# Softmax denominators in an attention phase: row sums over 64 partitions by one product, and their reciprocals on VectorE

## The chip, the cores and the metric
One Trainium2 chip, one of its cores. The metric is the device time of one execution of the whole program in microseconds (us), as the median of several runs.

## The reference, cut to what matters
Two blocks of a network on a sequence of 2048 tokens. The second block normalises x, projects it to q (8 heads of 64), k and v (2 heads of 64 each, shared by 4 query heads), gates and a convolution branch. The context of 256 tokens gives further keys and values, so each query sees 2304 keys. The change touches only this part:

```
s = jnp.einsum('bqkgd,bskd->bkgqs', qblk, k).astype(jnp.float32) * scale
pr = jax.nn.softmax(s, axis=-1).astype(v.dtype)
return jnp.einsum('bkgqs,bskd->bqkgd', pr, v)
```

All is float32. The softmax is taken as exp(s - max), weighted sum of v, and at the end a division by the sum of the exponentials (the denominator).

## The kernel before, in words
The program runs five phases one after the other, with a barrier between them: modulation, a gated linear attention block, the projections, `attention` (L1440) and the output. The change lies in `attention` alone.

The work of `attention` is 32 steps, one for a query head and a block of TB = 512 queries. A step goes over its 2304 keys in NKT = 18 turns of 128 keys. For step i, each engine runs a `body` of its own, whose instructions stand in an order written by hand, and semaphores tie the engines together:

- TensorE (`body`, L1623): each turn kt makes scores for 128 keys and 512 queries by two products (L1630, L1631) into one of three score banks. Between turns stand groups of other work. `piece` (L1590) makes four products of the scores of the NEXT step in the other orientation, in tokens by keys, only to find each query's maximum; there are 20 pieces in a step, five for each 128 queries (four of 512 keys and one of 256), and they stand in groups of four at the turns that PIECES_OF_TURN names. Pieces use 64 rows of the array each, so that two lie side by side. `weigh` (L1605) multiplies the exponentials with v into bank O, even keys into partitions 0 to 63 and odd ones into 64 to 127, three calls at each of the turns 9 and 14 and at turn 2 of the next step. `sum_den` (turn 5) and `spread_reciprocal` (turn 7) belong to the step before; `max_row` (turn 15) turns the maxima into a row.
- ScalarE takes the exponential of each turn's scores into p_f (L1694), copies half of O (L1682), rounds q and moves the row of maxima.
- VectorE finds maxima: `reduce` (L1726) reads one piece's bank and writes one column. Of the four banks M a group of pieces fills all; piece p waits, if p is even, until max(p - 2, 0) pieces of its step are reduced (`mx_read`, in `piece`). So the third piece of a group (p = 10 in the group at turn 9) waits for the whole group before it (p = 4 to 7). VectorE also adds the last of the sums of exponentials (L1743, L1747) and ends a step: `add_o` adds the two halves of O, `invert` takes the reciprocal, `finish` (L1762) multiplies and frees the output tile for a store by the SyncE queue.
- GpSimd adds the exponentials over the turns into den, seven tiles of 128x1024 a step by six additions (L1575).

Denominators before: `sum_den` has four products with a column of ones (L1613), one for each 128 queries, with the denominators in partitions and one column; `invert` (L1756) takes the reciprocal of 128x4 values; `spread_reciprocal` (L1620) turns each column, broadcast, into a row over 128 partitions with four transposes into O; `finish` reads that from O. The first `weigh` of a step waits for `o_done`, since O is free only when `finish` has read it.

Of the kernel before, what the change touches and what calls it, by code (L numbers as in the profile page):

```python
# [10 lines left out]
ALU = mybir.AluOpType  # L11
# [4 lines left out]
P = 128  # L16
SEQ, D = 2048, 1024
KT = D // P
TB = 512
NB = SEQ // TB  # L20
NT = TB // P
EPS = 1e-6
UP = 1
# [895 lines left out]
HD, NQH, NKV = 64, 8, 2  # L919
# [520 lines left out]
def attention(nc, d, keep):  # L1440
# [10 lines left out]
    STEPS = NKV * GROUP_STEPS  # L1451
    PIECES = [(qt, n) for qt in range(NT) for n in range(-(-KEYS // TB))]
    NP = len(PIECES)

    PIECES_OF_TURN = [0, 0, 4, 0, 4, 0, 0, 0, 0, 4, 4, 0, 0, 0, 4, 0, 0, 0]
    TURN_PIECES = [list(range(sum(PIECES_OF_TURN[:kt]), sum(PIECES_OF_TURN[:kt + 1]))) for kt in range(NKT)]
    assert sum(PIECES_OF_TURN) == NP
    with ExitStack() as ctx:
        sb, ps, sem = pools(nc, ctx, "att")
        ident = keep["ident"]  # L1460
# [4 lines left out]
        ones = sb("ones", [P, P])  # L1465
# [7 lines left out]
        p_f = sb("p_f", [P, NKT, TB])  # L1473
        den = [sb(f"den{s}", [P, 2, TB]) for s in range(2)]
        o_hi, o_out = sb("o_hi", [HD, TB]), sb("o_out", [HD, TB])
        recip = sb("recip", [P, NT])
        S = [ps(f"bank_s{i}", [P, TB]) for i in range(SBANKS)]
        M = [ps(f"bank_m{i}", [P, TB]) for i in range(MBANKS)]
        O = ps("bank_o", [P, TB])
# [7 lines left out]
            sem(n) for n in ("mx_done", "mx_read", "m_done", "mz_done", "row_done", "row_read"))  # L1487
        s_done, p_done, den_pool, den_dve, pv_done = (
            sem(n) for n in ("s_done", "p_done", "den_pool", "den_dve", "pv_done"))
        den_sum, o_hi_done, recip_done, r_row, o_sum, o_done, o_stored = (  # L1490
            sem(n) for n in ("den_sum", "o_hi_done", "recip_done", "r_row", "o_sum", "o_done", "o_stored"))

        def need(eng, semaphore, n):

            if isinstance(n, int) and n <= 0:
                return
            eng.wait_ge(semaphore, UP + n)
# [19 lines left out]
        with nc.Block() as block:  # L1517
# [60 lines left out]
            @block.tensor  # L1578
            def _(pe):
                def piece(i, s, g, p):  # L1580

                    qt, n = PIECES[p]
                    width = min(TB, KEYS - TB * n)
                    rows = slice(HD * (p % 2), HD * (p % 2 + 1))
                    if p == 0:
                        pe.wait_ge(q_hi_done, UP + i + 1)
                        need(pe, row_read, i)
                    if p % 2 == 0:
                        need(pe, mx_read, i * NP + max(p - MBANKS + 2, 0))
                    pe.matmul(M[p % MBANKS][:, 0:width], q_c[s][rows, P * qt:P * (qt + 1)], k_a[g][rows, TB * n:TB * n + width],  # L1590
                              start=True, stop=True).then_inc(mx_done, 1)

                def max_row(i):

                    pe.wait_ge(mz_done, UP + i + 1)
                    for qt in range(NT):
                        last = pe.transpose(M[0][0:HD + 1, P * qt:P * (qt + 1)], mz[:, qt, :], ident[:])
                    last.then_inc(row_done, 1)

                def weigh(i, s, g, j):  # L1600
                    pe.wait_ge(p_done, UP + i * NKT + 2 * j + 2)
                    if j == 0:
                        need(pe, o_done, i)
                    for half in range(2):
                        last = pe.matmul(O[HD * half:HD * (half + 1), :], v[g][:, 2 * j + half, :], p_f[:, 2 * j + half, :],  # L1605
                                         start=(j == 0), stop=(j == NPR - 1))
                    last.then_inc(pv_done, 1)

                def sum_den(i, s):
                    pe.wait_ge(den_dve, UP + (i + 1) * DVE_ADDS)  # L1610
                    pe.wait_ge(o_sum, UP + i + 1)
                    for qt in range(NT):
                        last = pe.matmul(O[:, qt:qt + 1], den[s][:, 0, P * qt:P * (qt + 1)], ones[:, 0:1], start=True, stop=True)  # L1613
                    last.then_inc(den_sum, 1)

                def spread_reciprocal(i):

                    pe.wait_ge(recip_done, UP + i + 1)
                    for qt in range(NT):
                        last = pe.transpose(O[:, P * qt:P * (qt + 1)], recip[:, qt:qt + 1].broadcast_to([P, P]), ident[:])  # L1620
                    last.then_inc(r_row, 1)

                def body(i, s, g, before, after):  # L1623
                    pe.wait_ge(row_read, UP + i + 1)
                    pe.wait_ge(q_lo_done, UP + i + 1)
                    pe.wait_ge(q_copied[s], UP + 32 * (i // 2) + 32)
                    for kt in range(NKT):
                        need(pe, p_done, i * NKT + kt - SBANKS + 1)
                        keys = slice(P * kt, P * (kt + 1))
                        pe.matmul(S[kt % SBANKS][:], k_a[g][:, keys], q_a[s][:], start=True, stop=False)  # L1630
                        pe.matmul(S[kt % SBANKS][:], k_b[g][:, keys], q_b[s][:], start=False, stop=True).then_inc(s_done, 1)  # L1631
                        if after is not None:
                            for p in TURN_PIECES[kt]:
                                piece(i + 1, 1 - s, after, p)
                        if kt == 2 and before is not None:
                            for j in GROUP_AT[kt]:
                                weigh(i - 1, 1 - s, before, j)
                        if kt in (9, 14):
                            for j in GROUP_AT[kt]:
                                weigh(i, s, g, j)  # L1640
                        if kt == 5 and before is not None:
                            sum_den(i - 1, 1 - s)
                        if kt == 7 and before is not None:
                            spread_reciprocal(i - 1)
                        if kt == 15 and after is not None:
                            max_row(i + 1)
                pe.wait_ge(ones_landed, UP + 16)
                pe.wait_ge(cleared, UP + 1)
                pe.wait_ge(k_hi_done, UP + 1)
                for p in range(NP):  # L1650
                    piece(0, 0, 0, p)
                max_row(0)
                pe.wait_ge(k_lo_done, UP + NKV)
                pe.wait_ge(v_landed, UP + 16 * NKV)
                pe.wait_ge(ones_row, UP + NKV)
                steps(pe, body)
                for j in GROUP_AT[2]:
                    weigh(STEPS - 1, 1, NKV - 1, j)
                sum_den(STEPS - 1, 1)
                spread_reciprocal(STEPS - 1)  # L1660

            @block.scalar
            def _(act):
# [50 lines left out]
            def _(dve):  # L1714
# [6 lines left out]
                def reduce(i, p):  # L1721
                    qt, n = PIECES[p]
                    dve.wait_ge(mx_done, UP + i * NP + p + 1)
                    if p == 0:
                        need(dve, m_done, i)
                    dve.reduce_max(mx[:, qt, n:n + 1], M[p % MBANKS][:, 0:min(TB, KEYS - TB * n)], AX_X).then_inc(mx_read, 1)  # L1726
# [25 lines left out]

                def invert(i):
                    dve.wait_ge(den_sum, UP + i + 1)
                    need(dve, r_row, i)
                    dve.reciprocal(recip[:], O[:, 0:NT]).then_inc(recip_done, 1)  # L1756

                def finish(i):
                    dve.wait_ge(r_row, UP + i + 1)
                    dve.wait_ge(o_sum, UP + i + 1)  # L1760
                    need(dve, o_stored, 16 * i)
                    dve.tensor_tensor(o_out[:], o_hi[:], O[0:HD, :], ALU.mult).then_inc(o_done, 1)  # L1762

                def body(i, s, g, before, after):
                    for kt in range(NKT):
                        if kt == 0 and after is not None:
                            split_q(i + 1, 1 - s)
                        if kt == 1 and before is not None:
                            add_den(i - 1, 1 - s, NPR - 1)
                            fold_den(i - 1, 1 - s)  # L1770
                        if kt == 4 and before is not None:
                            add_o(i - 1)
                        for n, p in enumerate(TURN_PIECES[kt]):
                            if after is not None:
                                reduce(i + 1, p)
                            if kt == 4 and n == 1 and before is not None:
                                invert(i - 1)
                        if kt == 4 and before is not None:
                            finish(i - 1)
                        if kt == 14 and after is not None:  # L1780
                            column(i + 1)
                        if kt == 17:
                            add_den(i, s, NPR - 2)
# [410 lines left out]
```

## Time and profile before
| | |
|---|---|
| median of 3 runs | 2878.21 us (2877.74 to 2882.36) |
| the profiled execution | 2884.46 us, of it a span of 2882.7 us |
| TensorE busy over the span | 90% |
| VectorE, ScalarE, GpSimd busy | 58%, 36%, 27% |
| the attention phase | about 1788 us to 2558 us of the span |
| one step in it | 23.3 us |

The span is the time between the first and the last instruction; what lies around it is 1.8 us. A timeline row has the start, the duration, engine, line, operation, out<-in, and the count of instructions merged in it; in brackets stands how long the engine was idle before, and what released it. A float32 product is two MATMUL records (a transpose is one), so `weigh` shows 12 records for six products. PEld is the load of weights, which runs beside PE.

### The profile page before, as it was taken

How to read it: one execution, taken by the hardware profiler on the slowest of the kernel's cores; microseconds unless marked ns; L12 is line 12 of the kernel's file. 1: busy time of each engine (PE TensorE's matmuls, PEld its weight loads, DVE VectorE, ACT ScalarE, POOL GpSimd, SP SyncE). 2: the span in 40 equal slices, each digit the busy share in tenths (PEclk: the TensorE clock that was granted, in tenths of full speed). 3: DMA queues.
4: the chain of work that ended last, by engine and by line, in shares of the span. 5: the costliest groups of instructions: out<-in, count | busy, mean ns of one | idle time of the engine just before them, and what ended most of it. 6: DMA issues, size and time to landing. Idle time of an engine off the chain costs nothing. (4 is left out here: it accounts for less than half of the span.)

```text
span 2882.7 us, 35232 instructions
## 1 busy us (share of the span) xinstructions
PE 2605.2 (90%) x11685; PEld 1754.7 (61%) x11685; DVE 1672.5 (58%) x2673; ACT 1044.2 (36%) x1830; POOL 765.5 (27%) x359
## 2 busy tenths in 40 slices
PE   8599899999999995699999993999999999947997
PEld 1177677777777774577777761444445544525776
DVE  0106542541542352488989866677777777746564
ACT  0234343343343331431313121445444444433332
POOL 0034321101111100003030112565556666631000
PEclk9799999999999997899999996899999999978999
DMA  8366578377567634557575654011111111033334
GB/s 318 106 220 196 184 246 287 126 251 257 189 215 249 215 126 159 194 182 261 186 252 185 225 177 101 23 28 29 32 29 28 28 28 28 24 121 114 120 131 146
DMA packets 233927, 433.54 MB, mean 150 GB/s; under 512 B 20513, under 2 KB 112151, under 8 KB 233552
## 3 DMA queue, kind: packets, MB, share of 16 engines
q1 hardware_dynamic: 207524, 337.48, 35.3%
q10 hardware_dynamic: 26284, 94.51, 9.5%
q8 instruction: 71, 1.16, 0.2%
q14 instruction: 48, 0.39, 0.0%
HBM read 326.77 MB, written 96.76 MB: 147 GB/s over the span
## 5 line engine op out<-in xcount | busy, mean ns | idle before, releaser
L1726 DVE TENSOR_REDUCE att_mx<-att_bank_m 128x1 f32<-128x512 f32 (+1 forms) x640 | 365.2, 629 | 114.1 <-PE att_bank_m L1590 110.3
L1694 ACT ACTIVATE att_p_f<-att_bank_s 128x512 f32<-128x512 f32 x576 | 317.9, 598 | 289.8 <-PE att_bank_s L1631 283.6
L456 PE MATMUL gla_bank_g<-gla_a_hi,gla_w_hi 128*128 128x512 f32 x1024 | 415.9, 406 | 5.2 <-POOL gla_w_lo L409 4.3
L456 PE MATMUL gla_bank_g<-gla_a_hi,gla_w_lo 128*128 128x512 f32 x1024 | 403.9, 394 | 0.0
L456 PE MATMUL gla_bank_g<-gla_a_lo,gla_w_hi 128*128 128x512 f32 x1024 | 403.5, 394 | 0.0
L1575 POOL TENSOR_TENSOR att_den<-att_den,att_p_f 128x1024 f32<-128x1024 f32 x160 | 378.9, 2368 | 36.3 <-ACT att_p_f L1694 24.2
L1342 DVE SCALAR_TENSOR_TENSOR proj_conv_acc<-proj_conv_in,proj_conv_w,proj_conv_acc 128x512 f32<-128x512 f32 (+1 forms) x480 | 353.1, 805 | 0.0
L1152 PE MATMUL proj_bank_g<-proj_u_hi,proj_w_hi 128*128 128x512 f32 x704 | 287.1, 408 | 3.7 <-DVE proj_u_lo L1330 3.7
L1152 PE MATMUL proj_bank_g<-proj_u_lo,proj_w_hi 128*128 128x512 f32 x704 | 274.3, 390 | 0.0
L1152 PE MATMUL proj_bank_g<-proj_u_hi,proj_w_lo 128*128 128x512 f32 x704 | 274.2, 389 | 0.0
L1605 PE MATMUL att_bank_o<-att_p_f,att_v 128*64 128x512 f32 x1152 | 270.1, 604 | 0.0
L1630 PE MATMUL att_bank_s<-att_q_a,att_k_a 128*128 128x512 f32 x576 | 258.7, 449 | 1.0 <-ACT att_q_b L1677 1.0
L1631 PE MATMUL att_bank_s<-att_q_b,att_k_b 65*128 65x512 f32 x576 | 230.3, 400 | 0.0
L456 PEld LDWEIGHTS gla_bank_g<-gla_a_hi,gla_w_hi 128*128 128x128 f32 x1024 | 195.1, 191 | 56.9 <-issue 14.3
L456 PEld LDWEIGHTS gla_bank_g<-gla_a_hi,gla_w_lo 128*128 128x128 f32 x1024 | 194.8, 190 | 42.8
L456 PEld LDWEIGHTS gla_bank_g<-gla_a_lo,gla_w_hi 128*128 128x128 f32 x1024 | 195.4, 191 | 38.2 <-issue 0.7
L1630 PEld LDWEIGHTS att_bank_s<-att_q_a,att_k_a 128*128 128x128 f32 x576 | 109.7, 190 | 137.0 <-issue 100.0
L827 DVE COPY gla_v_tok<-gla_bank_t 128x512 f32<-128x512 f32 x32 | 22.1, 691 | 260.7 <-PE gla_bank_t L563 260.7
L1152 PEld LDWEIGHTS proj_bank_g<-proj_u_hi,proj_w_hi 128*128 128x128 f32 x704 | 132.2, 188 | 55.3 <-issue 24.4
L1590 PE MATMUL att_bank_m<-att_k_a,att_q_c 64*128 64x512 f32 (+1 forms) x640 | 122.1, 435 | 47.9 <-ACT att_k_a L1666 44.9
L1605 PEld LDWEIGHTS att_bank_o<-att_p_f,att_v 128*64 128x64 f32 x1152 | 74.5, 137 | 146.0 <-issue 96.5
L402 POOL TENSOR_TENSOR gla_w_lo<-gla_w_raw,gla_w_hi 128x1024 fp32r<-128x1024 f32 x22 | 54.9, 2495 | 394.3 <-ACT gla_w_hi L622 394.3
(325 smaller groups left out, 4032.5 us busy)
## 6 DMA issues: line engine op xcount, KB each, us to landing
gla_w_hi<-scratch_w_hi SPq DMA_DIRECT2D x96, 512.0 KB, 4.2
gla_w_lo<-scratch_w_lo SPq DMA_DIRECT2D x96, 512.0 KB, 5.6
proj_w_hi<-scratch_w_hi ACTq DMA_DIRECT2D x90, 512.0 KB, 3.8
proj_w_lo<-scratch_w_lo ACTq DMA_DIRECT2D x90, 512.0 KB, 4.7
scratch_w_hi<-gla_w_hi SPq DMA_DIRECT2D x54, 512.0 KB, 4.4
scratch_w_lo<-gla_w_lo SPq DMA_DIRECT2D x54, 512.0 KB, 5.5
mod_wslab<-in_ada_w SPq DMA_DIRECT2D x6, 2048.0 KB, 11.3
mod_wslab<-in_w_mod SPq DMA_DIRECT2D x6, 2048.0 KB, 8.0
```

The lines of the kernel that those rows point to most:

```text
L402: pool.tensor_tensor(w2_lo[:], w_raw[m % 2][:], w2_hi[:].bitcast(F32), ALU.subtract).then_inc(w2_rest, 1)
L456: last = pe.matmul(banks[s % 2][:], w[:, k, :], a[:, k, :], start=(k == 0 and n == 0), stop=(k == KT - 1 and n == 2))
L827: dve.tensor_copy(v_tok[:, :, tok(j)], T[j % 2][:].rearrange("p (t i) -> p t i", t=NT)).then_inc(v_copied, 1)
L1152: last = pe.matmul(G[j % 2][:], w[:, k, :], a[half][:, k, :], start=(k == 0 and n == 0), stop=(k == KT - 1 and n == 2))
L1342: dve.scalar_tensor_tensor(acc, src, conv_w[:, c, k:k + 1], acc, ALU.mult, ALU.add).then_inc(taps, 1)
L1575: pool.tensor_tensor(den[s][:], pair(0) if j == 1 else den[s][:], pair(j), ALU.add).then_inc(den_pool, 1)
L1590: pe.matmul(M[p % MBANKS][:, 0:width], q_c[s][rows, P * qt:P * (qt + 1)], k_a[g][rows, TB * n:TB * n + width], start=True, stop=True).then ...
L1605: last = pe.matmul(O[HD * half:HD * (half + 1), :], v[g][:, 2 * j + half, :], p_f[:, 2 * j + half, :], start=(j == 0), stop=(j == NPR - 1))
L1630: pe.matmul(S[kt % SBANKS][:], k_a[g][:, keys], q_a[s][:], start=True, stop=False)
L1631: pe.matmul(S[kt % SBANKS][:], k_b[g][:, keys], q_b[s][:], start=False, stop=True).then_inc(s_done, 1)
L1694: act.activation(p_f[:, kt, :], S[kt % SBANKS][:], ACT.Exp, scale=float(HD) ** -0.5).then_inc(p_done, 1)
L1726: dve.reduce_max(mx[:, qt, n:n + 1], M[p % MBANKS][:, 0:min(TB, KEYS - TB * n)], AX_X).then_inc(mx_read, 1)
```

## The change
The sum over the 128 partitions of den is now one product with 64 columns of ones: every one of 64 partitions of O gets all 512 denominators as a row. The reciprocal is taken on this 64x512 tile, from O into an SBUF tile of that shape, and `finish` multiplies two SBUF tiles. The transposes are gone, and O is free for the next `weigh` once the reciprocal has read it (`recip_done` in place of `o_done`). The group of four pieces that stood at turn 4 stands at turn 5, directly ahead of the new product; the reciprocal stands between the second and the third reduction of that group, as before.

```diff
-    PIECES_OF_TURN = [0, 0, 4, 0, 4, 0, 0, 0, 0, 4, 4, 0, 0, 0, 4, 0, 0, 0]
+    PIECES_OF_TURN = [0, 0, 4, 0, 0, 4, 0, 0, 0, 4, 4, 0, 0, 0, 4, 0, 0, 0]
...
-        recip = sb("recip", [P, NT])
+        recip = sb("recip", [HD, TB])
...
                     if j == 0:
-                        need(pe, o_done, i)
+                        need(pe, recip_done, i)
...
-                    for qt in range(NT):
-                        last = pe.matmul(O[:, qt:qt + 1], den[s][:, 0, P * qt:P * (qt + 1)], ones[:, 0:1], start=True, stop=True)
-                    last.then_inc(den_sum, 1)
-
-                def spread_reciprocal(i):
-
-                    pe.wait_ge(recip_done, UP + i + 1)
-                    for qt in range(NT):
-                        last = pe.transpose(O[:, P * qt:P * (qt + 1)], recip[:, qt:qt + 1].broadcast_to([P, P]), ident[:])
-                    last.then_inc(r_row, 1)
+                    pe.matmul(O[0:HD, :], ones[:, 0:HD], den[s][:, 0, :], start=True, stop=True).then_inc(den_sum, 1)
...
-                        if kt == 7 and before is not None:
-                            spread_reciprocal(i - 1)
...
-                    need(dve, r_row, i)
-                    dve.reciprocal(recip[:], O[:, 0:NT]).then_inc(recip_done, 1)
+                    need(dve, o_done, i)
+                    dve.reciprocal(recip[:], O[0:HD, :]).then_inc(recip_done, 1)
...
-                    dve.wait_ge(r_row, UP + i + 1)
+                    dve.wait_ge(recip_done, UP + i + 1)
...
-                    dve.tensor_tensor(o_out[:], o_hi[:], O[0:HD, :], ALU.mult).then_inc(o_done, 1)
+                    dve.tensor_tensor(o_out[:], o_hi[:], recip[:], ALU.mult).then_inc(o_done, 1)
...
-                            if after is not None:
-                                reduce(i + 1, p)
-                            if kt == 4 and n == 1 and before is not None:
+                            if after is None:
+                                continue
+                            reduce(i + 1, p)
+                            if kt == 5 and n == 1 and before is not None:
                                 invert(i - 1)
-                        if kt == 4 and before is not None:
+                        if kt == 5 and before is not None:
+                            if after is None:
+                                invert(i - 1)
                             finish(i - 1)
```

On TensorE, in a step in the middle of the phase, from the scores of turn 4 on, the order was this before (att_bank_s are scores, att_bank_m pieces, att_bank_o is O):

```order
L1630 MATMUL att_bank_s<-att_q_a,att_k_a 128x512
L1631 MATMUL att_bank_s<-att_q_b,att_k_b 128x512
L1590 MATMUL att_bank_m<-att_k_a,att_q_c 128x256
L1590 MATMUL att_bank_m<-att_k_a,att_q_c 128x512 x3
L1630 MATMUL att_bank_s<-att_q_a,att_k_a 128x512
L1631 MATMUL att_bank_s<-att_q_b,att_k_b 128x512
L1613 MATMUL att_bank_o<-att_ones,att_den 128x1 x4
L1630 MATMUL att_bank_s<-att_q_a,att_k_a 128x512
L1631 MATMUL att_bank_s<-att_q_b,att_k_b 128x512
L1630 MATMUL att_bank_s<-att_q_a,att_k_a 128x512
L1631 MATMUL att_bank_s<-att_q_b,att_k_b 128x512
L1620 MATMUL att_bank_o<-ident_sb,att_recip 128x128 x4
```

and in the changed kernel, from the scores of turn 5 on, it is:

```order
L1621 MATMUL att_bank_s<-att_q_a,att_k_a 128x512
L1622 MATMUL att_bank_s<-att_q_b,att_k_b 128x512
L1590 MATMUL att_bank_m<-att_k_a,att_q_c 128x256
L1590 MATMUL att_bank_m<-att_k_a,att_q_c 128x512 x3
L1612 MATMUL att_bank_o<-att_den,att_ones 64x512
L1621 MATMUL att_bank_s<-att_q_a,att_k_a 128x512
L1622 MATMUL att_bank_s<-att_q_b,att_k_b 128x512
L1621 MATMUL att_bank_s<-att_q_a,att_k_a 128x512
L1622 MATMUL att_bank_s<-att_q_b,att_k_b 128x512
```

The four small products and the four transposes have become one product, directly behind the pieces and ahead of the scores of turn 6.

On VectorE the same stretch stood so before:

```order
L1747 TENSOR_TENSOR att_den<-att_den 128x512
L1726 TENSOR_REDUCE att_mx<-att_bank_m 128x1 x4
L1751 TENSOR_TENSOR att_o_hi<-att_bank_o,att_o_hi 64x512
L1726 TENSOR_REDUCE att_mx<-att_bank_m 128x1 x2
L1756 RECIPROCAL att_recip<-att_bank_o 128x4
L1726 TENSOR_REDUCE att_mx<-att_bank_m 128x1 x2
L1762 TENSOR_TENSOR att_o_out<-att_o_hi,att_bank_o 64x512
```

and now:

```order
L1735 TENSOR_TENSOR att_den<-att_den 128x512
L1714 TENSOR_REDUCE att_mx<-att_bank_m 128x1 x4
L1739 TENSOR_TENSOR att_o_hi<-att_bank_o,att_o_hi 64x512
L1714 TENSOR_REDUCE att_mx<-att_bank_m 128x1 x2
L1744 RECIPROCAL att_recip<-att_bank_o 64x512
L1714 TENSOR_REDUCE att_mx<-att_bank_m 128x1 x2
L1750 TENSOR_TENSOR att_o_out<-att_o_hi,att_recip 64x512
```

The places are the same; the reciprocal is of another shape, with two reductions of the group behind it.

## Rows read from the trace of the kernel before

**Rows 1.** Busy time over a stretch: PE, PEld, DVE, ACT, POOL, then granted clock
```profile
1811.00:2555.00 744.00, 734.47 (x3408) 367.78 (x3406) 559.91 (x896) 364.80 (x664) 452.64 (x192) 0.99 0.11 27
```

**Rows 2.** Timeline of one step, turns 4 to 10, PE and DVE
```profile
1952.21 0.72 PE L1590 MATMUL att_bank_m<-att_k_a,att_q_c 64*128 64x256 f32 x4
...
1953.44 0.95 PE L1613 MATMUL att_bank_o<-att_ones,att_den 128*128 128x1 f32 x8
...
1954.25 0.48 PE L1630 MATMUL att_bank_s<-att_q_a,att_k_a 128*128 128x512 f32 x1
...
1954.42 0.18 DVE L1756 RECIPROCAL att_recip<-att_bank_o 128x4 f32<-128x4 f32 x1 [0.78 <-PE att_bank_o L1613]
1954.52 1.28 DVE L1726 TENSOR_REDUCE att_mx<-att_bank_m 128x1 f32<-128x512 f32 x2
...
1955.04 0.39 PE L1631 MATMUL att_bank_s<-att_q_b,att_k_b 65*128 65x512 f32 x1
...
1955.27 0.60 PE L1620 MATMUL att_bank_o<-ident_sb,att_recip 128*128 128x128 f32 x4
1955.60 0.19 PEld L1630 LDWEIGHTS att_bank_s<-att_q_a,att_k_a 128*128 128x128 f32 x1
...
1956.72 0.73 PE L1590 MATMUL att_bank_m<-att_k_a,att_q_c 64*128 64x512 f32 x4
...
1957.38 2.79 PE L1605 MATMUL att_bank_o<-att_p_f,att_v 128*64 128x512 f32 x12
...
1958.29 0.14 PEld L1605 LDWEIGHTS att_bank_o<-att_p_f,att_v 128*64 128x64 f32 x2 [0.29 <-issue]
1958.72 0.14 PEld L1605 LDWEIGHTS att_bank_o<-att_p_f,att_v 128*64 128x64 f32 x2 [0.29 <-issue]
...
1960.11 0.50 PE L1630 MATMUL att_bank_s<-att_q_a,att_k_a 128*128 128x512 f32 x1
```

**Rows 3.** Groups of VectorE by shape: busy us, mean ns of one
```profile
L1756 DVE RECIPROCAL att_recip<-att_bank_o 128x4 f32<-128x4 f32 x32 | 5.9, 183 | 26.6 <-PE att_bank_o L1613 26.6
L162 DVE COPY cols<-mod_ps_cols 128x128 f32<-128x128 f32 x1 | 0.3, 292 | 11.6 <-PE mod_ps_cols L136 11.6
L1726 DVE TENSOR_REDUCE att_mx<-att_bank_m 128x1 f32<-128x256 f32 x128 | 53.3, 416 | 4.3 <-PE att_bank_m L1590 0.5
L1726 DVE TENSOR_REDUCE att_mx<-att_bank_m 128x1 f32<-128x512 f32 x512 | 327.9, 682 | 109.8 <-PE att_bank_m L1590 109.8
```

**Rows 4.** Timeline of TensorE around three pauses in an earlier phase
```profile
337.70 1.02 PE L594 MATMUL gla_bank_t<-ident_sb,gla_xrc 128*128 128x128 f32 x4 [2.45 <-DVE gla_xr L880]
...
354.94 0.76 PE L456 MATMUL gla_bank_g<-gla_a_hi,gla_w_hi 128*128 128x512 f32 x1 [2.03 <-POOL gla_w_lo L409]
355.50 0.63 PE L456 MATMUL gla_bank_g<-gla_a_lo,gla_w_hi 128*128 128x512 f32 x1
355.93 0.63 PE L456 MATMUL gla_bank_g<-gla_a_hi,gla_w_lo 128*128 128x512 f32 x1
...
601.35 0.63 PE L594 MATMUL gla_bank_t<-ident_sb,gla_xrc 128*128 128x128 f32 x4 [1.85 <-DMA gla_xrc<-in_x]
```

**Rows 5.** TensorE in stretches behind those pauses: busy, then granted clock
```profile
337.90:341.30 3.40, 3.40 (x11) 0.51 0.26 79
341.30:344.70 3.40, 3.40 (x16) 1.00 0.77 203
355.00:358.40 3.40, 3.40 (x8) 0.51 1.09 351
602.00:605.40 3.40, 3.40 (x16) 1.00 1.06 377
```

**Rows 6.** Timeline at the end of the phase, the last step's denominators
```profile
2556.96 0.68 DVE L1762 TENSOR_TENSOR att_o_out<-att_o_hi,att_bank_o 64x512 f32<-64x512 f32 x1 [1.21 <-PE att_bank_o L1620]
```

**Rows 7.** Timeline of GpSimd's additions and a small VectorE operation beside one
```profile
1965.41 2.35 POOL L1575 TENSOR_TENSOR att_den<-att_den,att_p_f 128x1024 f32<-128x1024 f32 x1
...
1966.51 1.28 DVE L1735 TENSOR_SCALAR att_mz<-att_m 128x4 f32<-128x4 f32 x1
```

More of the change, by code:

```diff
@@ L1489, in attention @@
             sem(n) for n in ("s_done", "p_done", "den_pool", "den_dve", "pv_done"))
-        den_sum, o_hi_done, recip_done, r_row, o_sum, o_done, o_stored = (
-            sem(n) for n in ("den_sum", "o_hi_done", "recip_done", "r_row", "o_sum", "o_done", "o_stored"))
+        den_sum, o_hi_done, recip_done, o_sum, o_done, o_stored = (
+            sem(n) for n in ("den_sum", "o_hi_done", "recip_done", "o_sum", "o_done", "o_stored"))
         def need(eng, semaphore, n):
@@ L1659, in _ @@
                 sum_den(STEPS - 1, 1)
-                spread_reciprocal(STEPS - 1)
             @block.scalar
```

## The prediction
> **What bounds the kernel now.** I read the busy times by engine first. Over the steady part of the attention phase TensorE is busy 734.5 of 744 us, VectorE 559.9, ScalarE 364.8, GpSimd 452.6, and the clock granted is 0.99 of full speed [rows 1]. So in this phase the order of work on TensorE sets the time. What TensorE no longer has to do comes off the end, 32 times; what another engine takes longer counts once TensorE has to wait for it. The second view is the timeline of one step [rows 2], which shows where the denominators stand between the scores, and when each wait would be met. The third are the groups of VectorE by shape [rows 3], for the price of the new reciprocal. The last are TensorE's pauses in an earlier phase and the clock behind them [rows 4, 5]. Below, all clock readings are those of the step in rows 2, whose four digits before the point I shorten (57.38 is 1957.38).
>
> **Removed from TensorE.** The four small products take a slot at 53.44 and the next scores start at 54.25: 0.81 us. The first score product behind such a change of work takes 0.48 in place of 0.39, so some 0.08 more: 0.89. The four transposes go from 55.27 to 55.60, 0.33, with the same 0.08 or so: 0.42. Together 1.31 us a step.
>
> **Added to TensorE.** One float32 product of 512 queries on 64 columns of ones has the form of one `weigh` product. Those run two side by side, and a pair of records starts every 0.43 us (58.29, 58.72); a product has two records, so a lone one occupies 0.86. The group of six takes from 57.38 to 60.11, 2.73, which is 6 x 0.43 and 0.15 for leaving that form of the array. So the new product costs 1.01 us. It cannot share the array with the pieces, which have 64 rows each where it has 128. Its weights are ones, 64 columns, and their load lies under the pieces.
>
> **Moved.** The group of pieces costs 0.66 us wherever it stands between scores (56.72 to 57.38), at turn 4 or 5, so the move alone is 0. ScalarE's exponentials are hidden: it is busy half the time, and four turns of scores in a row (6 to 9) are what turns 11 to 14 have already. TensorE alone would gain 1.31 - 1.01 = 0.3 us a step.
>
> **The times of the new order.** The four score products from 54.25 to 55.27 take 1.02 with the one 0.08: a turn of scores is 0.47. The pieces start one turn later than before, 52.21 + 0.47 = 52.68, and the product for the denominators at 53.34. The last of six `weigh` products ends 2.79 behind the first one's start, four slots of 0.43 less is 1.07 for a lone one: it ends at 54.41. The reciprocal starts then, where it did before (54.42). Scores of turns 6 to 9 follow from 54.35 on, and the pieces of turn 9 can start at 56.4, against 56.72 before.
>
> **The reciprocal.** This is the term that decides. The 128x4 one took 183 ns. A copy from PSUM of 128 columns took 292 [rows 3], and a reduction takes 682 for 512 columns and 416 for 256, so 1.04 ns a column; the copy's fixed part is 292 - 133 = 159 ns. The reciprocal is 24 ns above that for four columns. If that is a fixed part of its own, 512 columns take 183 + 508 x 1.04 = 0.71 us. If each column costs it, the price is 24/4 = 6.0 ns a column, and 512 take 0.16 + 3.07 = 3.23 us. With the reduction's fixed part (682 - 533 = about 150) in place of the copy's it is 33/4 = 8.25 ns and 4.37 us. I keep 0.71 and 4.4 as the ends and take 3.23: an engine that streams every other operation at the same fixed part has no reason to pay 24 ns once, and a copy out of PSUM is its nearest relative. 
>
> **What it holds up.** Two reductions stand behind the reciprocal on VectorE, those of the third and fourth piece of its group (1.28 us at 54.52). VectorE's next instruction starts 0.08 before the reported end of one (54.42 and 54.52 against 0.18). At turn 9 TensorE runs two pieces, and for the third it waits until all four of the group of turn 5 are reduced: 54.41 + R - 0.08 + 1.28 + 0.05 for the signal = 55.66 + R. The last two pieces take 0.44 of the 0.66, so `weigh` starts at 56.10 + R, against 57.38 before. At R = 1.0 us the reciprocal begins to hold up TensorE beyond its own gain, at 1.28 the change is even, and at 3.23 the step is 56.10 + 3.23 - 57.38 = 1.95 us longer. The wait of the first `weigh` for the reciprocal itself (57.6) is over by then, and moving it from `o_done` to `recip_done` gains nothing. VectorE has 5.9 us of idle time in a step of 23.3 [rows 1], so it catches up behind turn 10. Steps 1 to 30 have denominators and pieces at once: 30 x 1.95 = 58 us.
>
> `finish` now has both inputs in SBUF. A small VectorE operation on SBUF started at 66.51 and took 1.28 us, until GpSimd's addition (65.41, 2.35 us) was over [rows 7]. So `finish` may take up to some 2 us more, and hold back the reductions of turn 9; these are wanted only at turn 10, some 3.5 us later. I take 0, and 0.5 us a step as the upper end.
>
> **The clock.** TensorE now pauses in each step: the first two pieces of turn 9 end at about 56.9, the third starts at 58.9, so 2.0 us. In the earlier phase pauses of 2.45 and 2.03 us were followed by 3.4 us at a granted clock of 0.51, which is the 1.2 GHz level, and then full clock again; one of 1.85 us was followed by 1.00 [rows 4, 5]. At the lower level score-like products start every 0.43 us (355.50, 355.93) in place of 0.23 (55.04, 55.27), so 3.4 us of it lose 3.4 x (1 - 0.23/0.43) = 1.6 us. The new pause lies between these cases; I take six falls in ten, with none and all as ends: 30 x 0.6 x 1.6 = 29 us.
>
> **The ends.** The last step of the loop has no pieces; there `weigh` at turn 9 waits for the reciprocal (57.6 against some 56.7): 1 us. At the phase's end `finish` stood 1.21 us idle behind a reciprocal of 0.18 [rows 6]; these 1.39 us become 3.2: 1.8 us. Together 3.
>
> **Sum.** 58 + 29 + 3 = 90 us. The profiled execution took 2884.5 us, so it would be 2974; the median of the runs lies 6.3 below it, and against that median I say 2968 us. Differences of under 0.2% (6 us) can't be told from no change.
>
> **Rivals.**
> *The reciprocal costs over 8 ns a column* (4.4 us). For it speak the reduction's fixed part and the page's rule; against it the copy's. `weigh` comes 3.1 us later, 30 x 3.1 = 93; the pause is then 3.1 us and the clock falls nearly every time, 30 x 0.9 x 1.6 = 43; ends 5. About 3019 us.
> *The pauses cost no clock*: they end before it falls, as that of 1.85 us did. 58 + 3 = 61 us, 2939.
> *The reciprocal streams like any other operation* (0.71 us) and the 24 ns are paid once. Then `invert` and the two reductions end at 56.4, in time for everything, TensorE's own 0.3 us comes off 31 times, and the end loses a chain of transposes for 0.5 us of reciprocal, 0.9 us: about 10 us faster, 2868. This is the case of the other sign; it decides below R = 1.28 us. Only the smallness of 24 ns speaks for it.
>
> **How the numbers follow.** My forecast (3 to 3.6 us for the reciprocal, some of the falls of clock) has 0.42; over 8 ns a column 0.24; no fall of clock 0.17; streaming 0.17. The last one makes nearly all of the chance of faster, 0.13, and of no change, 0.04 (a gain of 10 us may come out as half); the other three make 0.83 of slower. The range need hold only these three: from 2925 (no falls and a reciprocal of 2.8 us, or so) to 3035 (4.4 us with a fall in each step).
>
> **What would show it.** In the changed kernel's profile: the reciprocal's mean time (0.7, 3.2 or 4.4 us); an idle time of TensorE ahead of the third piece of turn 9, released by VectorE's reduction, about 2 us in 30 steps; two MATMUL records of 64 columns and 0.43 us apart in place of eight and four; a granted clock in the phase under 0.99, near 0.95; and steps of 26 to 27 us in place of 23.3. The prediction is wrong if the reciprocal takes under 1.3 us, if the reductions come to stand elsewhere, or if the pause is followed by no or by many more low stretches of the clock.

## The result, and the profile after

The changed kernel takes 2982.03 us (median of 4 runs, 2980.59 to 2988.76) against 2880.07 us: 1.036 times the time before, with an interval of 1.034 to 1.038, so 102 us slower. The forecast was 2968, with a range of 2925 to 3035. The profiled execution has a span of 2987.0 us against 2882.7, 104.3 more.

VectorE's groups in the changed kernel, by shape (busy us, mean ns of one, idle before):

```profile
L1744 DVE RECIPROCAL att_recip<-att_bank_o 64x512 f32<-64x512 f32 x32 | 107.2, 3349 | 12.4 <-PE att_bank_o L1612 12.4
...
L1750 DVE TENSOR_TENSOR att_o_out<-att_o_hi,att_recip 64x512 f32<-64x512 f32 x32 | 46.2, 1443 | 0.1
```

The reciprocal answers to the 183 ns of [rows 3]. With 183 ns for 4 columns and 3349 for 512, a column costs 3166/508 = 6.2 ns; the forecast had 6.0 and 3.23 us.

One step, on TensorE and VectorE, from the pieces of turn 5 to the end of the pieces of turn 10 (it answers to [rows 2]):

```profile
1966.28 0.73 PE L1590 MATMUL att_bank_m<-att_k_a,att_q_c 64*128 64x256 f32 x4
...
1966.94 1.07 PE L1612 MATMUL att_bank_o<-att_den,att_ones 128*64 128x512 f32 x2
1967.94 0.50 PE L1621 MATMUL att_bank_s<-att_q_a,att_k_a 128*128 128x512 f32 x1
1968.05 3.35 DVE L1744 RECIPROCAL att_recip<-att_bank_o 64x512 f32<-64x512 f32 x1 [0.33 <-PE att_bank_o L1612]
...
1970.18 0.49 PE L1590 MATMUL att_bank_m<-att_k_a,att_q_c 64*128 64x512 f32 x2
1971.32 1.21 DVE L1714 TENSOR_REDUCE att_mx<-att_bank_m 128x1 f32<-128x512 f32 x2
1972.46 1.45 DVE L1750 TENSOR_TENSOR att_o_out<-att_o_hi,att_recip 64x512 f32<-64x512 f32 x1
1972.59 0.50 PE L1590 MATMUL att_bank_m<-att_k_a,att_q_c 64*128 64x512 f32 x2 [1.92 <-DVE att_mx L1714]
1973.02 4.49 PE L1605 MATMUL att_bank_o<-att_p_f,att_v 128*64 128x512 f32 x12
```

The new product keeps the next scores away from 66.94 to 67.94, 1.00 us (forecast 1.01). The first two pieces of turn 9 run at 70.18; the third waits at 72.59 for VectorE's reductions, which stand behind the reciprocal: TensorE is idle for 1.92 us (forecast 2.0). Then the six weighing products last 4.49 us against 2.79 in [rows 2]. The clock in these stretches (span, PE busy, PEld, DVE, ACT, POOL, then granted clock), with the mean over the phase first:

```profile
1850.00:2640.00 790.00, 726.05 (x2886) 318.95 (x2888) 641.49 (x847) 335.75 (x623) 425.00 (x177) 0.95 0.10 24
1965.00:1973.00 8.00, 6.08 (x24) 2.98 (x22) 6.66 (x7) 4.13 (x8) 6.73 (x3) 1.00 0.00 0
1973.00:1976.40 3.40, 3.40 (x12) 1.06 (x12) 3.03 (x5) 0.00 (x0) 3.04 (x2) 0.62 0.18 39
```

Full speed up to the pause, and a mean of 0.62 in the 3.4 us behind it, a mixture of the 1.2 and the 2.4 GHz level. I call such a stretch a fall of the clock. The record of the granted clock has one of 3.4 us in 26 of the 30 steps with a pause, and one more in the last step of the loop, which has no pieces and where the weighing waits 1.45 us for the reciprocal. The mean of 0.95 over 790 us says about the same (0.05 x 790 / 0.5 = 79 us at the lower level, 23 stretches, where the record has 25 in that window).

The start of turn 9's pieces, from step to step, gives the length of a step with a fall and of one without:

```profile
1997.24 0.49 PE L1590 MATMUL att_bank_m<-att_k_a,att_q_c 64*128 64x512 f32 x2
...
2024.24 0.50 PE L1590 MATMUL att_bank_m<-att_k_a,att_q_c 64*128 64x512 f32 x2
...
2049.59 0.50 PE L1590 MATMUL att_bank_m<-att_k_a,att_q_c 64*128 64x512 f32 x2
```

From 1970.18 to 1997.24 it is 27.06 us, from 2024.24 to 2049.59 it is 25.35, and 23.33 before. So a step is 2.02 us longer by the wait, and a fall costs 1.71 us more. 30 x 2.02 = 61 and 26 x 1.71 = 44 us give 105 us. The trace has the same: from the reciprocal of the first step with pieces to that of the last step of the loop, 30 steps on, it is 802.90 us (1833.03 to 2635.93) against 698.12 (1837.79 to 2535.91), 104.8 more. That is the difference of the spans within a microsecond.

### The profile page after: what moved, and what is told of

Same layout as the page of the kernel before. It is cut to its first block and busy times, and to the rows that moved or that the text cites. A ratio compares the mean times of both kernels' runs of the same rounds, so it can differ in the third digit from the quotient of the medians.

```text
span 2987.0 us, 34591 instructions
## 1 busy us (share of the span) xinstructions
PE 2652.3 (89%) x11365; PEld 1731.6 (58%) x11365; DVE 1792.1 (60%) x2673; ACT 1037.3 (35%) x1830; POOL 772.3 (26%) x359
## 5 line engine op out<-in xcount | busy, mean ns | idle before, releaser
L1682 ACT ACTIVATE att_p_f<-att_bank_s 128x512 f32<-128x512 f32 x576 | 311.1, 599 | 402.9 <-PE att_bank_s L1622 397.1
L1575 POOL TENSOR_TENSOR att_den<-att_den,att_p_f 128x1024 f32<-128x1024 f32 x160 | 387.4, 2422 | 132.5 <-ACT att_p_f L1682 120.4
L1605 PE MATMUL att_bank_o<-att_p_f,att_v 128*64 128x512 f32 x1152 | 313.2, 686 | 1.5 <-DVE att_recip L1744 1.5
L1590 PE MATMUL att_bank_m<-att_k_a,att_q_c 64*128 64x512 f32 (+1 forms) x640 | 131.3, 448 | 105.7 <-DVE att_mx L1714 60.9
L1605 PEld LDWEIGHTS att_bank_o<-att_p_f,att_v 128*64 128x64 f32 x1152 | 83.7, 153 | 171.3 <-issue 137.8
```

The lines of the kernel that those rows point to most:

```text
L1575: pool.tensor_tensor(den[s][:], pair(0) if j == 1 else den[s][:], pair(j), ALU.add).then_inc(den_pool, 1)
L1682: act.activation(p_f[:, kt, :], S[kt % SBANKS][:], ACT.Exp, scale=float(HD) ** -0.5).then_inc(p_done, 1)
```

## The experiments

All times are medians of several runs. The experiments were run in three sets, each on one chip and beside runs of the kernel before (2879.6 to 2880.2 us in each set). Ratios are to those runs, with their interval in brackets.

**A copy in place of the reciprocal.**

```diff
-                    dve.reciprocal(recip[:], O[0:HD, :]).then_inc(recip_done, 1)
+                    dve.tensor_copy(recip[:], O[0:HD, :]).then_inc(recip_done, 1)
```

> The reciprocal of 64x512 is replaced by a copy of the same shape, at the same place; the output is multiplied by the denominators in place of divided. Theory A (the reciprocal's 3.35 us on VectorE, ahead of two reductions of maxima, is the whole loss): a copy takes 0.69 us, the pause of TensorE in turn 9 goes, the granted clock in the phase is back at 0.99, and what is left is TensorE's own gain of 0.3 us a step: 2869 us, 2863 to 2876. Rival B (the new product, the moved group of pieces or the new waits cost by themselves): 2890 us or more.

Measured: 2876.81 us, ratio 0.999 (0.998 to 1.000), and the clock is back at full speed:

```profile
1830.00:2500.00 670.00, 662.20 (x2832) 300.72 (x2829) 562.23 (x839) 326.08 (x605) 421.58 (x174) 1.00 0.11 28
```

The loss is gone with the reciprocal; the rest of the change costs nothing on balance. But the gain left is 3 us, hardly clear of the noise, and not 11. A row of the same kernel shows what took part of it, in turns 6 to 9:

```profile
1975.66 0.40 PE L1621 MATMUL att_bank_s<-att_q_a,att_k_a 128*128 128x512 f32 x1
...
1976.20 0.19 PEld L1621 LDWEIGHTS att_bank_s<-att_q_a,att_k_a 128*128 128x128 f32 x1 [0.34 <-ACT att_p_f L1682]
1976.20 0.50 PE L1621 MATMUL att_bank_s<-att_q_a,att_k_a 128*128 128x512 f32 x1
```

The scores of turn 9 start 0.54 us behind those of turn 8, in place of 0.47, and take 0.50 in place of 0.40, since TensorE's stream was broken. What they wait for is ScalarE's exponential of turn 6, which ended at 1976.15. Some 0.15 of the 0.3 us a step are given back here (a step is 23.18 us against 23.33 before), so that 31 x 0.15 = 5 us of gain are left.

**The move of the pieces alone**, in the kernel before.

```diff
-    PIECES_OF_TURN = [0, 0, 4, 0, 4, 0, 0, 0, 0, 4, 4, 0, 0, 0, 4, 0, 0, 0]
+    PIECES_OF_TURN = [0, 0, 4, 0, 0, 4, 0, 0, 0, 4, 4, 0, 0, 0, 4, 0, 0, 0]
...
-                            if kt == 4 and n == 1 and before is not None:
+                            if kt == 5 and n == 1 and before is not None:
                                 invert(i - 1)
-                        if kt == 4 and before is not None:
+                        if kt == 5 and before is not None:
```

> The kernel before with only the group of pieces moved from turn 4 to turn 5, ahead of the four small products, and the reductions with it. Theory A: a group costs 0.66 us wherever it stands, so 2880 us, 2875 to 2886. Rival B (the move costs, by the reductions of turn 5 coming closer to the pieces of turn 9): over 2890 us, 0.4 us or more a step.

Measured: 2880.13 us, ratio 1.0002 (0.999 to 1.001). The move is worth nothing, as forecast.

**The reciprocal behind all four reductions.**

```diff
-                            if kt == 5 and n == 1 and before is not None:
+                            if kt == 5 and n == 3 and before is not None:
                                 invert(i - 1)
```

> The changed kernel with the reciprocal behind all four reductions of its group in place of between the second and third. Theory A (the third piece of turn 9 waits for reductions that stand behind the reciprocal): that wait goes, the first weighing product waits for the reciprocal itself in its place, 1.3 us later than in the kernel before against 2.0 now, and the pause is 1.5 us, too short for the clock to fall: 30 x 1.3 + 3 = 42 us over before, 2922 us; 2960 if the clock still falls. Rival C (it is the reciprocal's length between product and weighing that counts, wherever it stands): no difference from the changed kernel, 2982 us.

Measured: 2949.41 us, ratio 1.024 (1.022 to 1.025). That is between the two theories' numbers. The timeline shows the wait where theory A puts it:

```profile
2012.40 3.34 DVE L1744 RECIPROCAL att_recip<-att_bank_o 64x512 f32<-64x512 f32 x1
2013.75 0.73 PE L1590 MATMUL att_bank_m<-att_k_a,att_q_c 64*128 64x512 f32 x4
2015.87 1.61 DVE L1750 TENSOR_TENSOR att_o_out<-att_o_hi,att_recip 64x512 f32<-64x512 f32 x1
2015.88 4.49 PE L1605 MATMUL att_bank_o<-att_p_f,att_v 128*64 128x512 f32 x12 [1.40 <-DVE att_recip L1744]
```

All four pieces now run together, and the first weighing product waits 1.40 us for the reciprocal. But the clock fell nevertheless, here at this very step, and in every second one: 15 of 30, and once more in the last step. Behind the next step's pause, at 2042.24, it stayed up (busy times, then granted clock):

```profile
2016.00:2019.00 3.00, 3.00 (x10) 1.05 (x11) 3.00 (x5) 0.00 (x0) 2.92 (x2) 0.55 0.00 0
2043.00:2047.00 4.00, 4.00 (x18) 1.68 (x15) 3.82 (x7) 0.60 (x1) 2.98 (x2) 1.00 0.15 33
```

My expectation that so short a pause would cost no clock was wrong. What I had compared it with was a lone pause of 1.85 us in dense work [rows 4]; here four pieces stand directly ahead of it. But that isn't the whole of it: steps beside each other have the same pause of 1.40 us behind the same four pieces, one with a fall and one without, so neither the pause's length nor the work just ahead of it decides alone. What does, these runs don't tell.

**The pause filled with work**, in the changed kernel and in the one above. Four score products whose results are overwritten stand where TensorE pauses.

```diff
                             for n, p in enumerate(TURN_PIECES[kt]):
+                                if kt == 9 and n == 2:
+                                    pe.wait_ge(p_done, UP + i * NKT + 8)
+                                    for _ in range(4):
+                                        pe.matmul(S[1][:], k_a[g][:, 0:P], q_a[s][:], start=True, stop=True)
                                 piece(i + 1, 1 - s, after, p)
```

> The changed kernel with four more score products, whose results are overwritten, between the second and the third piece of turn 9, where TensorE pauses. They take 0.95 us of the 1.9. Theory A (a pause of about 2 us makes the clock fall, and 26 falls of 3.4 us cost 1.6 us each): the pause is cut to about 1 us, no falls, 2982 - 42 = 2940 us, 2934 to 2948, with more work done. Rival D (the falls cost nothing, since TensorE has time to spare, or don't come of this pause): 2982 us or more.

> The kernel of e3_behind (reciprocal behind all four reductions) with four more score products, results overwritten, between the pieces of turn 9 and the first weighing product, where TensorE pauses for 1.4 us. Theory A: what e3_behind had over its expected 2922 us is its 15 falls of the clock, 1.6 us each; with the pause cut to about 0.5 us they go, and the time is 2949 - 24 = 2925 us, 2918 to 2931. Rival I (the falls there cost nothing, and the reciprocal's end is simply later than I worked out): 2949 us.

Measured: 2941.89 us in the changed kernel (ratio 1.021, 1.019 to 1.023) and 2925.61 us with the reciprocal behind the reductions (1.016, 1.014 to 1.018). Expected were 2940 and 2925. With four products more a step the one is 40 us faster and the other 24. In the timeline the pause is cut from 1.92 to 0.79 us in the one and from 1.40 to 0.28 in the other. The same stretch of each, first the one with the filled pause of the changed kernel:

```profile
1850.00:2590.00 740.00, 709.91 (x2980) 326.10 (x2976) 637.44 (x846) 331.00 (x614) 422.67 (x175) 1.00 0.10 26
```

and the kernel with the reciprocal behind, before its pause was filled and after:

```profile
1850.00:2590.00 740.00, 692.51 (x2832) 313.21 (x2831) 637.40 (x840) 326.35 (x606) 419.22 (x174) 0.97 0.10 26
```

```profile
1850.00:2590.00 740.00, 724.17 (x3032) 337.21 (x3032) 649.34 (x848) 338.09 (x628) 431.94 (x179) 1.00 0.10 26
```

No fall is left in the steps of either. A step of the changed kernel with its pause filled is 25.36 us long, like the 25.35 of its steps without a fall. So the falls come of the pauses and each costs 40/27 = 1.5 us in the one kernel and 24/16 = 1.5 in the other. The kernel with the reciprocal behind has, without its falls, 2926 us, near the 2922 that the wait alone was worked out to give. Of the 102 us of the change 62 are the wait and 40 the clock.

**Half the columns.** The reciprocal takes 256 columns; the other 256 queries are multiplied by a tile of ones set at the start.

```diff
+                pool.memset(recip[:], 1.0).then_inc(cleared, 1)
...
-                    dve.reciprocal(recip[:], O[0:HD, :]).then_inc(recip_done, 1)
+                    dve.wait_ge(cleared, UP + 1)
+                    dve.reciprocal(recip[:, 0:TB // 2], O[0:HD, 0:TB // 2]).then_inc(recip_done, 1)
```

> The changed kernel with the reciprocal of the first 256 columns only; the other 256 queries are not divided. Theory A (each column costs 6.2 ns, from 183 ns for 4 and 3349 for 512, and a step gets longer by what the reciprocal lasts beyond 1.3 us): it takes 1.76 us, weighing starts 0.5 us later than in the kernel before, the pause is 0.5 us and the clock does not fall: 30 x 0.5 + 1 = 16 us over before, 2895 us, 2888 to 2900. Rival E (the loss is in proportion to the reciprocal's length): half of 102 us, 2931 us.

```profile
L1746 DVE RECIPROCAL att_recip<-att_bank_o 64x256 f32<-64x256 f32 x32 | 56.0, 1750 | 12.5 <-PE att_bank_o L1613 12.5
```

Measured: 2891.71 us, ratio 1.004 (1.003 to 1.006). The reciprocal takes 1.75 us, on the line of 6.2 ns a column. Half the length brings 12 us of loss, an eighth of 102, and not a half: the cost begins beyond the point where VectorE has time to spare. The pause is 0.3 to 0.5 us here and no fall follows it, so the clock's part begins beyond that.

**Versions that keep the gain.** If the reciprocal costs only by its place, it can be moved to where VectorE is idle. What holds it there is bank O, which the next weighing needs. In the first version ScalarE copies the denominators out of O at turn 5, and the reciprocal is taken in four parts behind the reductions of turns 5, 9 and 10. In the second, the 512 queries also lie as two halves of 256 in the two halves of the partitions. The third moves the product of the second to turn 7. In all three `finish` stands at turn 14. In short, with the lines of the second:

```diff
-                        need(pe, recip_done, i)
+                        need(pe, den_copied, i)
...
-                    pe.matmul(O[0:HD, :], ones[:, 0:HD], den[s][:, 0, :], start=True, stop=True).then_inc(den_sum, 1)
+                    for h in range(2):
+                        last = pe.matmul(O[HD * h:HD * (h + 1), 0:HT], ones[:, 0:HD], den[s][:, 0, HT * h:HT * (h + 1)], start=True, stop=True)
+                    last.then_inc(den_sum, 1)
...
+                    act.activation(den_c[:], O[:, 0:HT], ACT.Copy).then_inc(den_copied, 1)
...
-                    dve.reciprocal(recip[:], O[0:HD, :]).then_inc(recip_done, 1)
+                    dve.reciprocal(recip[:], den_c[:]).then_inc(recip_done, 1)
```

> A version meant to keep the change's gain: ScalarE copies the denominators out of bank O after turn 5, which frees it, and VectorE takes the reciprocal from SBUF in four parts of 128 columns behind the reductions of turns 5 (two), 9 and 10, and finishes at turn 14. Theory A (the reciprocal costs only by standing between TensorE's groups of pieces): no pause, no falls; TensorE's gain of 0.3 us a step is halved by ScalarE, whose exponentials are late in the four turns 6 to 9, as the run with a copy showed: 2875 us, 2869 to 2880. Rival F (VectorE, with 3.3 us more in a step, becomes the bound or delays the maxima of turn 14): over 2890 us.

> As the version before, but the two halves of the 512 queries lie in the two halves of the partitions: two products of 256 columns side by side, a reciprocal of 128x256 (1.76 us) behind the reductions of turn 5, sum and finish on 128x256, two stores. Theory A: the product costs 0.43 + 0.15 in place of 1.01 us, so TensorE's gain is 0.73 us a step, less 0.15 for ScalarE in turns 6 to 9: 31 x 0.58 = 18 us, 2862 us, 2855 to 2868. Rival F: over 2885 us.

> As v2_folded, with the products for the denominators at turn 7 in place of 5, the copy with them, and the reciprocal behind the reductions of turn 9. Theory G (ScalarE's exponentials hold up turn 9 when four turns stand in a row): the run of four is broken into two and two, the 0.15 us comes back, and entering the product from scores costs 0.1: 2860 us, 2853 to 2866, no slower than v2_folded. Rival H (the wait seen at turn 9 is not ScalarE's): 0.1 us a step slower than v2_folded, 3 us more.

Measured: 2878.53 us (ratio 0.999, 0.998 to 1.000), 2865.66 (0.995, 0.994 to 0.996) and 2866.41 (0.995, 0.994 to 0.997). The first is within 2 us of the copy's 2876.8, with all of the division done: 3.7 us of reciprocal in a step cost nothing that can be told from noise in this place. Of the second the rows of its reciprocal and finish (by shape):

```profile
L1762 DVE RECIPROCAL att_recip<-att_den_c 128x256 f32<-128x256 f32 x32 | 56.1, 1753 | 3.4 <-ACT att_den_c L1683 2.5
...
L1768 DVE TENSOR_TENSOR att_o_out<-att_o_hi,att_recip 128x256 f32<-128x256 f32 x32 | 14.7, 460 | 0.1
```

The same denominators on 128 partitions take half the time, and with two products of 256 columns side by side the next scores start 0.58 us behind them in place of 1.00. The gain of 14.5 us is 3.5 less than expected. Between the second and the third nothing can be told apart: the wait at turn 9 is gone in the third's trace, and what it gave back went, as far as the timeline shows, into one more change between forms of products. Theory G is neither borne out nor refuted by the time.

**One wait more.** The trace of the second version has GpSimd's additions later, and a small operation of VectorE behind them, which the row of maxima needs:

```profile
1976.66 7.28 POOL L1580 TENSOR_TENSOR att_den<-att_den,att_p_f 128x1024 f32<-128x1024 f32 x3
...
1982.59 1.38 DVE L1739 TENSOR_SCALAR att_mz<-att_m 128x4 f32<-128x4 f32 x1
...
1984.03 0.65 PE L1602 MATMUL att_bank_m<-ident_sb,att_mz 128*65 128x128 f32 x4 [0.32 <-DVE att_mz L1739]
```

```diff
-                    dve.tensor_scalar(mz[:, :, HD], m[:], -1.0, None, ALU.mult).then_inc(mz_done, 1)
...
+                    act.activation(mz[:, :, HD], m[:], ACT.Copy, scale=-1.0).then_inc(mz_done, 1)
```

> v2_folded with the sign of the column of maxima changed by ScalarE (behind the exponential of turn 14) in place of VectorE. Theory J (on VectorE this small operation on SBUF waits for the end of GpSimd's addition, 1.4 us for 128x4 elements, and max_row at turn 15 waits for it, 0.3 us in the kernel before and 0.4 in v2_folded, with a restart of TensorE's stream of 0.2 or so): the wait goes, 31 x 0.4 = 12 us, 2854 us, 2848 to 2861. Rival K (something else sets the start of max_row, or ScalarE's exponential of turn 15 gets as late): 2866 us or more.

```profile
L1684 ACT ACTIVATE att_mz<-att_m x32: 208/209/211, 1793.5 to 2493.6; 128x4 f32<-128x4 f32 x32
```

Measured: 2852.57 us, ratio 0.991 (0.989 to 0.993). This is the second version with the change of sign taken by ScalarE. ScalarE takes 0.21 us for it, and the wait at turn 15 is gone. This is the fastest version of all, 27 us under the kernel before and 129 under the changed one.

## Why the prediction was right

- **The reciprocal.** 6.0 ns a column from the 24 ns by which the 128x4 row lay above a copy; measured 6.2, at 4, 256 and 512 columns. The small excess of a tiny operation was the whole effect. It was a choice between two fixed parts, 159 and 150 ns, and these 9 ns made the difference between 3.23 and 4.37 us; the runs bear out the first (183 - 4 x 6.2 = 158 ns). The case of over 8 ns falls. With it falls the 4.3 us that the prediction estimated from the Trainium skill, "VectorE: DVE Perf Modes", section "Walkthrough: the 8-slice pipeline in each mode", by taking the repeat count of 8 as eight cycles a column: the trace does not agree, 6.2 ns are about six cycles of the page's 0.96 GHz. The streaming reciprocal of the rival that was faster falls too; the run with a copy is that rival's mechanism, and gave 2877 where I had 2868.
- **TensorE's own gain.** The product costs the 1.01 us worked out. The 0.3 us a step came only to about half: "ScalarE's exponentials are hidden" was wrong for four turns in a row between two groups of pieces. The turns 11 to 14 that I compared them with have a wait for ScalarE as well, only shorter. In the changed kernel this gain doesn't count, since the third piece of turn 9 waits anyway.
- **What it holds up.** The third piece of turn 9 was 1.92 us late against 1.95 and 2.0 forecast, the step 2.02 us longer: 61 us against 58.
- **`finish`.** It takes 1.44 us on average against 0.68 before. Both inputs lie in SBUF, and it ends some 0.5 us behind the end of the GpSimd addition that runs when it starts (2051.88 to 2053.34, with the addition's end at 2052.80). At the end, where GpSimd is idle, it takes 0.68. In the changed kernel TensorE waits for nothing behind it, so the 0 of the sum holds.
- **The clock.** This term was mis-sized: six falls in ten steps, 29 us, against 26 in 30 and 44 us by the timeline, or 40 by the filled run. The price of a fall, 1.6 us, was right (1.7 by the timeline, 1.5 by the filled runs). Its frequency was a choice between two ends, not worked out from anything, and the truth lay near the upper one. Most of what the forecast of 2968 lacks to 2982 is here; 3 us are the wait, and 2 the base, since the kernel before has a median of 2880 us beside the change and had 2878 in the rows ahead of it.
- **The range.** 2982 lies in it; the rival without any fall (2939) is what the filled run gives, 2942. The upper end of 3035 does not come out of its own terms: 4.4 us and a fall in each step make 93 + 48 + 5 = 146 us, some 3024. And VectorE's idle time in [rows 1] is 5.8 us a step, not 5.9, which changes nothing.

## What to carry to other kernels

Price a reciprocal by its columns on a partition, never by its elements: 128x4 is nearly free, 64x512 costs 3.35 us, and the layout that saved 0.3 us on the bounding engine put that on a chain which it waits for. Ask of a long instruction on an engine with time to spare what stands behind it in its order, and what holds it in that place; here a copy that freed the bank, and a place behind the reductions, made the same reciprocal free. And count a new pause of the matmul engine twice, once for itself and once for the clock behind it.

## What the runs showed of the hardware

- VectorE's reciprocal: 183 ns for 4 columns, 919 for 128, 1.75 us for 256 and 3.35 us for 512. At 256 columns 64 partitions out of PSUM (1750 ns) and 128 out of SBUF (1753) are alike. A copy of 64x512 takes 0.68.
- A pause of 1.40 us, with four products of 64 rows ahead of it, was followed by 3.4 us at the lower clock in every second step, where a lone one of 1.85 us in the kernel before was not. A pause of 1.92 us was followed by it in 26 of 30. In the last step of the loop a pause of some 1.46 us was followed by it in the changed kernel, and not in the one with filled pauses. Four products whose results are overwritten, inside the pause, removed all falls and made the kernels 40 and 24 us faster.
- A VectorE operation with two SBUF inputs (64x512) took 0.68 us alone, and 1.4 to 1.7 us where it started within one of GpSimd's additions. What counted was how much of the addition was left: with half the columns it started 0.08 us before the end of one (2047.41, 2047.49) and took 0.67, with the next addition running beside its rest. In the last version the 128x256 one took 1.73 us in place of 0.43. The reciprocal out of SBUF, which has one input, took its 1.75 us beside the additions and without them.
